# Prompt attention of a hybrid encoder: value products by head pairs on two column halves, score products by two fp32r passes

## The reference

```python
sc = jnp.einsum('bcqhd,bckhd->bchqk', chunked(q), k_band).astype(jnp.float32) * (d ** -0.5)
sc = jnp.where(valid[None, :, None, None, :], sc + bias[None, None], -jnp.inf)      # mixer A
p = jax.nn.softmax(sc, axis=-1).astype(v.dtype)
o = jnp.einsum('bchqk,bckhd->bcqhd', p, v_band)
...
_, idx = lax.top_k(isc, k_sel)                                                      # mixer B
sc = jnp.einsum('bqhd,bqkhd->bqhk', q, kg).astype(jnp.float32) * (q.shape[-1] ** -0.5)
sc = jnp.where(valid[:, :, None, :], sc, -jnp.inf)
```

## Time and profile before

| | us |
|---|---|
| median of three runs (lowest, highest) | 2633.05 (2632.14, 2633.63) |
| the profiled execution | 2633.2 |
| its span, first to last instruction | 2631.5 |
| PE, DVE, ACT, POOL busy in the span | 2504.1, 1316.3, 986.7, 510.4 |
| prompt attention, second reduction of (0,0) to the end of (1,7) | 326.0 |

### The profile page before, as it was taken

How to read it: one execution, slowest core, us unless ns; L and a number is a source line. 1 busy time by engine, 2 the same in 40 slices (tenths; PEclk the granted TensorE clock), 3 DMA queues, 4 the chain that set the end, 5 groups by cost and what they waited for, 6 DMA issues and landing times. The chain is left out here.

```text
span 2631.5 us, 41101 instructions
## 1 busy us (share of the span) xinstructions
PE 2504.1 (95%) x17116; PEld 2270.4 (86%) x17116; DVE 1316.3 (50%) x2297; ACT 986.7 (37%) x1671; POOL 510.4 (19%) x369
## 2 busy tenths in 40 slices
PE   6999999999998999998799998798999999999997
PEld 6999999988887889997687776477999999988886
DVE  6433333234554379897677764434633333334454
ACT  6333332333432232324566654423433333323332
POOL 0234343400000112382000001000343333310000
PEclk9999999999998999999999999999999999999999
DMA  3122222266552123132202136741122222245553
GB/s 128 51 84 67 85 67 83 75 228 218 199 191 85 35 69 103 35 103 93 83 25 72 59 129 217 271 169 49 51 67 85 67 85 67 84 162 205 202 212 115
DMA packets 153112, 294.34 MB, mean 112 GB/s; under 512 B 14032, under 2 KB 90456, under 8 KB 152928
## 3 DMA queue, kind: packets, MB, share of 16 engines
q1 hardware_dynamic: 146688, 268.12, 29.9%
q0 software_dynamic: 6240, 23.59, 2.5%
HBM read 237.26 MB, written 61.78 MB: 114 GB/s over the span
## 5 line engine op out<-in xcount | busy, mean ns | idle before, releaser
L819 DVE TENSOR_TENSOR f_dl<-f_raw_d,f_dh 128x2048 fp32r<-128x2048 f32 x66 | 151.3, 2293 | 273.7 <-ACT f_dh L634 273.7
L634 ACT ACTIVATE f_dh<-f_raw_d 128x2048 fp32r<-128x2048 f32 x66 | 126.5, 1916 | 321.2 <-PE f_pV L151 286.6
L584 ACT ACTIVATE f_gh<-f_pX 128x256 f32<-128x256 f32 x120 | 49.2, 410 | 311.8 <-PE f_pX L151 311.8
L151 PE MATMUL f_pX<-f_xop,f_u_slo 128*128 128x256 f32 x504 | 149.2, 296 | 0.0
L150 PE MATMUL f_pX<-f_xop,f_u_shi 128*128 128x256 f32 x504 | 149.2, 296 | 0.0
L149 PE MATMUL f_pX<-f_xop,f_u_shi 128*128 128x256 f32 x504 | 149.2, 296 | 0.0
L149 PE MATMUL w_pw<-i_hi,r_T_hi 128*128 128x256 f32 (+1 forms) x504 | 145.3, 288 | 2.6 <-PEq L367 2.6
L2014 ACT ACTIVATE t_sc<-t_sc,t_small 128x640 f32<-128x640 f32 (+8 forms) x136 | 100.0, 735 | 122.1 <-DVE t_small L1943 110.0
L150 PE MATMUL w_pw<-i_lo,r_T_hi 128*128 128x256 f32 (+1 forms) x504 | 144.8, 287 | 0.0
L151 PE MATMUL w_pw<-i_hi,r_T_lo 128*128 128x256 f32 (+1 forms) x504 | 144.2, 286 | 0.0
L584 ACT ACTIVATE f_tu<-f_pX 128x256 f32<-128x256 f32 x126 | 51.7, 410 | 244.5 <-PE f_pX L151 244.5
(11 more groups left out here) (377 smaller groups left out, 8135.8 us busy)
## 6 DMA issues: line engine op xcount, KB each, us to landing
f_raw_d<-in_ffn_w_down SPq DMA_DIRECT2D x66, 1024.0 KB, 5.0
hid<-f_gh SPq DMA_DIRECT2D x22, 1152.0 KB, 9.2
f_raw_h<-hid SPq DMA_DIRECT2D x66, 384.0 KB, 5.5
f_u_raw<-in_ffn_w_up SPq DMA_DIRECT2D x21, 1024.0 KB, 6.4
f_g_raw<-in_ffn_w_gate SPq DMA_DIRECT2D x20, 1024.0 KB, 5.3
proj<-w_stage POOLq DMA_DIRECT2D x12, 1152.0 KB, 5.6
i_raw<-in_w_in SPq DMA_DIRECT2D x12, 1024.0 KB, 5.1
...
```

The source lines that it names most:

```text
L151: return pe.matmul(out, a[1], b[0], start=False, stop=last, skip_group_check=goes_on)
L584: act.activation(dst, by_tile(pX[:, c, 0:N[c]]), ACT.Copy).then_inc(s_copy, 1)
L634: act.activation(d_hi[slot(q)][:], raw_d[slot(q)][:], ACT.Copy).then_inc(s_dhi, 1)
L819: dve.tensor_tensor(d_lo[slot(q)][:], raw_d[slot(q)][:], d_hi[slot(q)][:].bitcast(F32), ALU.subtract)
```

## The change

Scores: keys and queries are split into high and low parts in fp32r. For each head the 128 rows of kS0 or kS1 hold the high part of its 64 features on one half and the low part on the other. The queries' 64 features stand twice, on both halves (q_hi, and their low part q_lo), so a pass with q_hi and a pass with q_lo give the whole product. Keys take two ACT and two DVE instructions, queries come in two halves of four heads, each with four transposes, an ACT copy and a DVE subtraction. The factor 1/8 moves from the queries to the reduction's scale, and the bias of mixer A is stored times 8. kS0 is a ring of 6 blocks, in the second half of the output's buffers.

Values: for each pair of heads the weights are 64 columns of v, the moving operand is pT (128 columns), and the two heads of a pair write to partitions 0 to 63 and 64 to 127 of po, so that the output comes out feature by row and isn't transposed. The reciprocals are spread by 8 matmuls with the identity into pm, ACT copies them to osb[0], DVE multiplies po by that into osb[1], and the split for the output projection reads osb[1].

The plan: keys of the next tile stand ahead of the turn of head 0 (before: behind the score in head 1), queries ahead of heads 4 and 6, values behind the turns of even heads for the two heads before, out (the reciprocals now) and the values of heads 6 and 7 in head 0 of the next tile, split in head 2. Zeroing of qT goes. Cached values of the first two sample items are loaded behind the last score, and some buffers of the sample part move.

The diff, cut to its core:

```diff
     for g, (x, t, h) in enumerate(heads):
         n = tiles.index((x, t))
-        if h == 4 and n + 1 < len(tiles):
-            plan.append(("queries",) + tiles[n + 1])
+        if h == 0 and n + 1 < len(tiles):
+            plan.append(("keys",) + tiles[n + 1])
+        if h in (4, 6) and n + 1 < len(tiles):
+            plan.append(("queries",) + tiles[n + 1] + (h // 2 - 2,))
+        if g == 1:
+            plan.append(("queries", 0, 0, 1))
         plan.append(("turn", g))
+        if h == 0 and g:
+            plan.append(("out",) + tiles[n - 1])
+        if h % 2 == 0 and g:
+            plan.append(("value", g - 2))
         if g + 2 < len(heads):
             plan.append(("score", g + 2))
-        if h == 1 and n + 1 < len(tiles):
-            plan.append(("keys",) + tiles[n + 1])
-        if g >= 1:
-            plan.append(("value", g - 1))
         if h == 2 and n >= 1:
-            plan.append(("out",) + tiles[n - 1])
+            plan.append(("split",) + tiles[n - 1])
...
+RING = LEFT // 2 + 2
+def key_chunks(x, t):
+    first, n = blocks_of(x, t)
+    cuts = [c for c in range(n) if c % 4 == 0 or x == 0 and (first + c) % RING == 0] + [n]
+    return [(a, b, (first + a) % RING if x == 0 else first + a) for a, b in zip(cuts, cuts[1:])]
...
-            todo_act, todo_dve = todo_act + n + 2, todo_dve + SHARE * n + 2
+            todo_act, todo_dve = todo_act + n + 4, todo_dve + SHARE * n + 3
...
 @block.sync
+                for e in range(2):
+                    sp.dma_start(q_rows(n, half).rearrange("p (h e d) -> p e h d", e=2, d=HD)[:, e],
+                                 proj_v[:, t, c:c + FW // 2].rearrange("p (h d) -> p h d", d=HD)).then_inc(s_rq[half], 16)
...
-                    sp.wait_ge(s_s, NP * H)
                     for s in range(2):
                         cached_keys(s)
-                        cached_values(s)
...
-            sp.wait_ge(s_o, NH)
             sp.wait_ge(s_s, NH)
-            new_values(0)
-            new_values(1)
+            for s in range(2):
+                cached_values(s)
+                new_values(s)
...
 @block.vector
-                    dve.tensor_tensor_reduce(out=sc_of(g, 0, n), in0=ps[g % 2][:, 0:n], in1=b, scale=-1.0, scalar=FIRST,
+                    dve.tensor_tensor_reduce(out=sc_of(g, 0, n), in0=ps[g % 2][:, 0:n], in1=b, scale=-HD ** -0.5, scalar=FIRST,
...
+                elif e[0] == "value" and heads[e[1]][2] == H - 2:
                     n = e[1] // H
-                    dve.wait_ge(s_o, e[1] + 1)
-                    dve_out(dve, None, n)
+                    dve.wait_ge(s_o, H * (n + 1))
+                    dve.wait_ge(s_ma, misc[("o",) + tiles_of[n]] + 1)
+                    dve.tensor_tensor(osb[:, 1, :], po[:], osb[:, 0, :], ALU.mult).then_inc(s_os, 1)
+                elif e[0] == "keys":
+                    x, t = e[1:]
+                    dve.wait_ge(s_ma, misc[("k", x, t)] + 1)
+                    for r in range(2):
+                        i = dve.tensor_tensor(keys_of(x, t, r, 1 - r), turned_keys(r), keys_of(x, t, r, r).bitcast(F32), ALU.subtract)
+                    i.then_inc(s_ml, 1)
+                elif e[0] == "queries":
+                    hs = slice(4 * e[3], 4 * e[3] + 4)
+                    dve.wait_ge(s_ma, misc[("q",) + e[1:]] + 1)
+                    dve.tensor_tensor(q_lo[:, hs, :], pm[:].rearrange("p (h c) -> p h c", c=P),
+                                      q_hi[:, hs, :].bitcast(F32), ALU.subtract).then_inc(s_ml, 1)
...
 @block.scalar
+                    for r in range(2):
+                        i = act.activation(keys_of(x, t, r, r), turned_keys(r), ACT.Copy)
+                    i.then_inc(s_ma, 1)
...
                             if e[1] >= 2:
-                                act.wait_ge(s_o, e[1] - 1)
+                                act.wait_ge(s_o, e[1] // 2 * 2)
                             act.activation(pT[:, e[1] % 2, b0 * P:(b0 + nb) * P], pt[u % 2][:, 0:nb * P], ACT.Copy).then_inc(s_pt[0], 1)
...
                 elif e[0] == "out":
                     m = misc[("o",) + e[1:]]
                     act.wait_ge(s_mf, m + 1)
+                    if e[1] * NP + e[2]:
+                        act.wait_ge(s_os, e[1] * NP + e[2])
+                    act.activation(osb[:, 0, :], pm[:], ACT.Copy).then_inc(s_ma, 1)
...
 @block.tensor
-                    for c in range(0, nb, 4):
-                        c1 = min(c + 4, nb)
-                        last = pe.matmul(ps[g % 2][:, c * P:c1 * P], qT[:, (x * NP + t) % 2, h, :],
-                                         kT[x][:, h // 2, (k0 + c) * P:(k0 + c1) * P], start=True, stop=True)
+                    for a, b, k in key_chunks(x, t):
+                        for q in (q_hi, q_lo):
+                            last = pe.matmul(ps[g % 2][:, a * P:b * P], q[:, h, :], key_rows(x, h, k, k + b - a),
+                                             start=q is q_hi, stop=q is q_lo)
...
-                    for u, _, _ in units[g]:
+                    for u, _, _ in units[g] + units[g + 1]:
                         wait_turned(pe, u)
                     for j in range(nb):
-                        last = pe.matmul(po[:, h * HD:(h + 1) * HD], pT[:, g % 2, j * P:(j + 1) * P],
-                                         v[x][:, k0 + j, h * HD:(h + 1) * HD], start=j == 0, stop=j == nb - 1)
-                    last.then_inc(s_o, 1)
+                        for r in range(2):
+                            last = pe.matmul(po[r * HD:(r + 1) * HD, h * HD:(h + 2) * HD], v[x][:, k0 + j, (h + r) * HD:(h + r + 1) * HD],
+                                             pT[:, (g + r) % 2, j * P:(j + 1) * P], start=j == 0, stop=j == nb - 1)
+                    last.then_inc(s_o, 2)
...
-                    pe.wait_ge(s_os, n + 1)
-                    pe_rows(pe, ("o",) + e[1:], osb[:, n % 2, :])
+                    pe.wait_ge(s_rc, n + 1)
+                    out = pe_misc(pe, ("o",) + e[1:])
+                    for h in range(H):
+                        r, cs = h % 2, slice(h // 2 * P, (h // 2 + 1) * P)
+                        last = pe.matmul(out[r * HD:(r + 1) * HD, cs], rec[:, n % 2, h:h + 1].broadcast_to([P, HD]), ident[:],
+                                         start=True, stop=True)
+                    last.then_inc(s_mf, 1)
```

150 lines of the change are left out of this document (91 added, 59 removed).

## The result

The changed kernel takes 2732.5 us, the kernel before beside it 2633.3: a ratio of 1.0377, 95% interval 1.0364 to 1.039. It is slower, as forecast, but by 99 us where 49 were forecast, and outside the range. The profiled execution has a span of 2727.5 us for 2631.5. The prompt attention takes 421.5 us, from the second reduction of tile (0,0) to the last multiplication, for 326.0: 95.5 of the 96.0 us. What lies before and behind it kept its length.

A forecast was written before the change was run, and what follows sets the result against it. The prompt stage was taken as PE-bound before; after, waits in program order give +39 us for tiles with n up to 4, +15 at n = 5, -5 for the last three: 2633 + 49 = 2682 us, range 2618 to 2708.

The forecast's parts named there:

- 1 to 3 us each: Sign: DVE idles this long before key lows, query lows and the multiply, released by ACT.
- Rival 4: Value passes on column halves don't run side by side: +58 us of PE, half on the walk, 2710; chance 0.03.
- the walk: Prompt tiles timed link by link in program order across PE, ACT and DVE: 375 us against 326, +49.
- time 0: PE ends its second score ... reciprocals to 4.55: Head of an n = 1 tile: PE waits at pm from 0.6, reciprocals end at 4.55; period 16.5 us.
- rival 3: PE's clock at its lower level in small tiles: +3 us for each of eight, 2706; chance 0.12.
- seam: A tile's first reduction to its third; at n = 5 walked with multiply to 8.96, reduction 2 with search step 11.0.
- a reduction (0.82) and its search step (1.25) follow every 2 to 3 us: n = 5 tile after reduction 2: DVE steps at this pace; PE ends the next tile's second score at 26.3.
- such a loop: Last tile, n = 8: exp, copies, values, score, reduction take 7.8 us for two heads; drain ends at 32.3.
- near 65%: Sign: PE's busy share of the prompt attention stretch in the profile after the change.
- Rival 1: Engines overlap better than walked, DVE bounds the stage: 293 plus at most 20 us, 2600 to 2620; chance 0.15.
- Rival 2: Large tiles gain more than walked, small ones lose as walked: 344 us, 2651; slower 0.17, no change 0.04.

The follow-up runs named there:

- e1: Changed kernel plus 128-column fp32 matmuls nobody reads, two ahead of each turn and ten ahead of each tile's spread reciprocals; 2707.0 us.
- e7: Changed kernel without the prompt's top-k search steps, except the last one of each of its two tiles; 2719.9 us.
- e16: Changed kernel with more pT buffers, value pairs behind even heads' scores (n up to 5), reciprocals in their own tile's head 7, keys behind head 1's score; 2682.0 us.
- e17: Kernel before with the value part of the change only, more pT buffers and the order of e16; 2643.3 us, ratio 1.004.

## Why the prediction was half right

**What held.** The stage loses by its waits in program order, not by work, and no engine is its bound. PE waits 47 us for the reciprocals, and DVE idles before the key lows, the query lows and the multiplication, released by ACT, as foreseen; before the multiplication it is 4.7 us a tile (70.9 in 15), where "1 to 3 us each" was said. At the full clock (e1) tile (1,0) takes 16.42 us, walked at 16.5. The prices of single operations, by form over the stage (busy us, mean ns, idle before):

```profile
L2236 PE MATMUL t_po<-t_pT,t_v 128*64 128x128 f32 x576 | 45.8, 312 | 0.9 <-ACT t_pT L2117 0.9
...
L2023 DVE TENSOR_TENSOR t_q_lo<-t_pm,t_q_hi 128x512 fp32r<-128x512 f32 x31 | 21.4, 690 | 14.1 <-ACT t_q_hi L2102 13.9
...
L2018 DVE TENSOR_TENSOR t_kS<-t_pm,t_kS 64x512 fp32r<-64x512 f32 x30 | 20.7, 689 | 16.4 <-ACT t_kS L2094 16.2
```

The subtractions cost the 0.69 us of the earlier trace rows, DVE's sum is 267 for 274, ACT's 225 for 226. The column halves do run side by side at full clock: 20 half passes, 1575.18 to 1576.43, are 1.25 us for ten slots with the change of width, where 1.10 + 0.09 were forecast. Rival 4 is out. A 512-column fp32r pass is followed by the next after 0.23 us (1576.76 to 1576.99 in the trace), as in the earlier trace rows; one of 128 columns after 0.06, my lower bound, where I had taken 0.12. The cached values stayed hidden.

**What failed: the walk was summed at full clock.** The step in the working's own words is "time 0: PE ends its second score ... reciprocals to 4.55", with PE's work at the prices of rows at 1.00, and the clock was set aside in rival 3: "+3 for each of the eight small tiles, 2706", chance 0.12. The clock fell in nearly all tiles, the large ones too (0.88 at n = 5), since the wait that the walk itself had put on PE came in every seam. e1 prices it at 24 us or more. The Trainium skill ("TensorE: Matmul & The Clock Gate", "Why this matters for your kernels") tells to avoid idle gaps between bursts, and the trace agrees: 0.69 while PE stands, 0.50 in the burst. Rival 3 was no rival, it was a term of the forecast. That its 24 us are e1's 24.0 is luck: it had all of them in the eight small tiles, where e1 got back 12.5.

**What failed: the large tiles were walked too short.** At full clock (e1) the tiles with n up to 4 sum to 157.2 us where I had 151.5; 2.6 of these 5.7 are (0,0)'s. Those with n from 5 up sum to 240.3 for 223.6, so 16.7 of the remaining 22.5 us are there. In "a reduction (0.82) and its search step (1.25) follow every 2 to 3 us" I let DVE set the pace behind the seam; e7 shows that it doesn't. The seam itself was right: from the second reduction to the third, (1,4) has 8.60 us in e1, walked at 8.96. From there to the next tile's second it has 19.65, walked at 17.3 (8.96 to 26.3). What sets the pace there is the loop of 5.86 us for two heads, with the value pair on one side of it and the high and low parts on the other: in e16, with the pair out, two heads still take 5.86, and in e17, without the parts as well, 5.09. The last tile was put at 32.3 us by such a loop and took 35.3, at clock 0.95; with e1's clock of 1.00 it took 35.5, so the clock is not its cause. Its loop of two heads was right (7.77 us in e1 from turn to turn, 7.8 forecast); the other 3 us lie at its head and in the drain, which the working did not write out.

The sum: 49 forecast, 24 clock, 16.7 large tiles, 5.7 small ones, together the 95.5 measured but for rounding.

**The other rivals.** PE's share of the stage, put near 65%, is 72% (305 of 421), its rows being longer at the lower clock. Rival 1 (DVE as the bound, 2600 to 2620) is out by the time itself, and e7 shows why. Rival 2 had large tiles at 22 and 24 us; they took 29 and 35.

**What stays open.** Why the fp32r scores still cost 39 us in e16 was read off one tile (the links of high and low parts on ACT and DVE), and not tried by taking those links away, nor was the clock's part in it separated. The parts of e1's gain that come from the matmuls' own cost were not separated; it makes 24 a lower bound, for this order of the plan.
